# Conformer and short-convolution decoder layer in float32: three gate units placed behind the convolutions, swish as one activation, LayerNorm over eleven units

## What is computed

```
z = rmsnorm(h, norm_g); proj = z @ w_in            # 9 blocks of 1024 columns
a_val, a_glu, a_gate, b_h, b_c, b_b, b_gate, m_a, m_b = split(proj)
u_a = a_val * sigmoid(a_glu)
c_a = layernorm(causal_dwconv31(u_a) + conv_a_b, ln_a_g, ln_a_b)
y_a = silu(c_a) * silu(a_gate)
y_b = b_b * causal_dwconv3(b_c * b_h) * silu(b_gate)
merged = sigmoid(m_a) * (y_a @ w_pa) + sigmoid(m_b) * (y_b @ w_pb)
y = rmsnorm(h + merged @ w_out, final_norm_g)       # and the convolutions' last rows
```

## Time and profile before

| | |
|---|---|
| median of 3 runs | 1204.2 us (1204.0 to 1205.83) |
| the profiled execution | 1199.34 us |
| its span, first to last instruction | 1197.4 us |
| mean granted TensorE clock | 0.951 |
| TensorE matmul busy | 1059.4 us, 88%, 7948 matmuls |
| VectorE busy | 808.6 us, 68% |
| ScalarE busy | 440.1 us, 37% |
| GpSimd busy | 594.5 us, 50% |
| moved by DMA | 212.24 MB, mean 177 GB/s |

### The profile page before, as it was taken

The page is one execution under the profiler, slowest core; times in us unless marked ns, Lnnn a source line. Parts: engine busy times, 40 slices in busy tenths (PEclk is TensorE's granted clock), DMA queues, the critical chain, the costliest instruction groups (busy, mean ns, idle before and its releaser), DMA issues.

```text
span 1197.4 us, 19916 instructions
## 1 busy us (share of the span) xinstructions
PE 1059.4 (88%) x7948; PEld 1026.6 (86%) x7948; DVE 808.6 (68%) x853; ACT 440.1 (37%) x679; POOL 594.5 (50%) x451
## 2 busy tenths in 40 slices
PE   5869999999999999999999899854969694997997
PEld 4869999999999999999999889854969694996885
DVE  6636867968868999898989675671283286445333
ACT  7343333334334333333333445532443152223221
POOL 2166556656566565666666455532555464455000
PEclk8879999999999999999999999987889897998999
DMA  7355576566667566665766988897767968565220
GB/s 254 104 138 134 133 193 167 147 164 171 146 159 175 145 171 161 159 164 135 177 148 149 246 248 244 257 294 252 180 189 222 269 178 251 162 214 176 89 88 38
DMA packets 217151, 212.24 MB, mean 177 GB/s; under 512 B 10751, under 2 KB 170623, under 8 KB 216020
## 3 DMA queue, kind: packets, MB, share of 16 engines
q1 hardware_dynamic: 192292, 165.87, 43.7%
q0 software_dynamic: 24768, 45.10, 21.1%
HBM read 131.83 MB, written 35.00 MB: 139 GB/s over the span
## 4 chain that ended last, share of the span: by engine, by line
PE 38%; DVE 22%; DMA 15%; issue 10%; POOL 4%; ACT 4%; SPq 3%; DVEq 0%; ACTq 0%; POOLq 0%
PE pp L1835 29%; PE pp L1989 8%; POOL wop L824 4%; DVE spare L1453 3%; DVE big L1442 3%; DMA sgb<-m_spill 3%; DMA big<-c_spill 2%; DMA ya_spill<-big 2%; DVE spare L1442 2%; DMA c_spill<-big 2%; DMA m_spill<-big 2%; DMA ga_spill<-big 1%; DVE big L1492 1%; ACT wop L893 1%; DMA big<-ya_spill 1%
## 5 line engine op out<-in xcount | busy, mean ns | idle before, releaser
L1835 PE MATMUL pp<-xop,wop 128*128 128x262 f32 (+1 forms) x7224 | 916.2, 290 | 105.4 <-ACT big L1053 43.1
L1835 PEld LDWEIGHTS pp<-xop,wop 128*128 128x128 f32 x7224 | 907.3, 194 | 112.2 <-issue 106.7
L824 POOL TENSOR_TENSOR wop<-ring,wop 128x512 fp32r<-128x512 f32 (+1 forms) x262 | 446.3, 1712 | 409.4 <-ACT wop L893 405.5
L893 ACT ACTIVATE wop<-ring 128x512 fp32r<-128x512 f32 (+1 forms) x262 | 181.8, 698 | 268.0 <-PE pp L1835 256.2
L1442 DVE SCALAR_TENSOR_TENSOR big<-big,cst 128x513 f32<-128x513 f32 x112 | 106.9, 955 | 0.4
L1989 PE MATMUL pp<-xop,wop 128*128 128x512 f32 x384 | 91.9, 402 | 6.6 <-DVE wop L1785 6.6
L1989 PEld LDWEIGHTS pp<-xop,wop 128*128 128x128 f32 x384 | 73.8, 193 | 24.5 <-issue 6.8
L1522 DVE TENSOR_TENSOR big<-big,pp 128x524 f32<-128x524 f32 (+1 forms) x43 | 29.9, 695 | 91.5 <-PE pp L1835 91.0
L1453 DVE SCALAR_TENSOR_TENSOR spare<-big,tap_sum,spare 128x512 f32<-128x512 f32 x112 | 83.8, 748 | 0.3
L1442 DVE SCALAR_TENSOR_TENSOR spare<-big,cst,spare 128x512 f32<-128x512 f32 x112 | 83.6, 747 | 0.0
L1349 DVE TENSOR_TENSOR xop<-big,xop 128x2064 fp32r<-128x2064 f32 (+1 forms) x21 | 55.3, 2639 | 24.7 <-ACT xop L919 24.6
(11 more groups left out here) (126 smaller groups left out, 700.1 us busy)
## 6 DMA issues: line engine op xcount, KB each, us to landing
ring<-in_w_in_dram SPq DMA_DIRECT2D x249, 256.0 KB, 3.4
ring<-ring POOLq DMA_DIRECT2D x172, 256.0 KB, 4.6
big<-c_spill SPq DMA_DIRECT2D x16, 516.0 KB, 5.2
ring<-in_w_pb_dram SPq DMA_DIRECT2D x28, 256.0 KB, 3.9
ring<-in_w_pa_dram SPq DMA_DIRECT2D x28, 256.0 KB, 3.9
big<-yb_spill SPq DMA_DIRECT2D x5, 1032.0 KB, 7.4
big<-ya_spill SPq DMA_DIRECT2D x5, 1032.0 KB, 12.7
yb_spill<-big SPq DMA_DIRECT2D x8, 516.0 KB, 5.4
```

The source lines that it names most:

```text
L824: G.tensor_tensor(wop[:, s0:s1, 1, :], raw, f(wop[:, s0:s1, 0, :]), ALU.subtract).then_inc(wlo, 1)
L893: A.activation(wop[:, s0:s1, 0, :], raw, ACT.Copy).then_inc(whi, 1)
L1835: last = T.matmul(out, wop[:, s, wp, P * k:P * (k + 1)], xop[s][:, xp, k, n * ch:n * (ch + 1)], start=(s in FRESH and k == 0 and m == 0), ...
```

## The change

- `agate` 1 to 3 leave their places behind `gate` 0, 1 and 2 and stand between `mix` 3 and `mix` 4. Units 1 to 24 are now the 24 units of the convolution blocks and 25 to 35 are eleven "late" units, n = 0 to 10: `mix` 0 to 3, `agate` 1 to 3, `mix` 4 to 7. All blocks use the former `TIGHT` table.
- Every swish is one ScalarE instruction with the function Silu; the VectorE multiplications by the sigmoid go.
- LayerNorm steps are placed by n from 0 to 8, with four `nrm` buffers for three and finer steps; the quarter loads of phase 1 stand at n = 9, in the order 2, 3, 0, 1. Operand steps of the `pb` and `pa` phases move earlier by one or two places, and in the first `pa` unit the merge stands behind `c12`.

```diff
     for j in range(K):
         UNITS += [("glu", j), ("short", j), ("gate", j)]
-        if j < 3:
-            UNITS += [("agate", j + 1)]
-    UNITS += [("mix", q) for q in range(K)]
+    LATE0 = len(UNITS)
+    UNITS += [("mix", q) for q in range(4)] + [("agate", m) for m in range(1, 4)] + [("mix", q) for q in range(4, 8)]
...
-        nrm = [cut(TOK * (2 + i), TOK) for i in range(3)]
+        nrm = [cut(TOK * i, TOK) for i in (2, 3, 4, 7)]
...
-        SPREAD = {"short": (2, 9, 11, 13), "gate": (13, 20, 22, 23), "agate": (25, 33, 35, 36), "end": (38, 44, 46, 48)}
-        TIGHT = {"short": (3, 13, 15, 17), "gate": (17, 25, 27, 29), "end": (31, 42, 44, 48)}
+        SPREAD = {"short": (3, 13, 15, 17), "gate": (17, 25, 27, 29), "end": (31, 42, 44, 48)}
...
-                if u == M + 6:
-                    spill_ya(7)
-                    for q in range(4):
-                        load_quad(1, q)
+                if n == 9:
+                    for q in (2, 3, 0, 1):
+                        load_quad(1, q)
+                if u == NZ + 1:
+                    for q in (2, 3, 0, 1):
+                        load_quad(2, q)
...
                 elif kind == "gate":
-                    act.wait_ge(ub_ready, 2 * i + 1)
-                    A.activation(half(g2, u, 0), src, ACT.Sigmoid).then_inc(bsig_ready, 1)
+                    A.activation(src, src, ACT.Silu).then_inc(bswish_ready, 1)
...
             def norm_swish(j):
-                row = nrm[(8 + j) % 3]
                 act.wait_ge(ys_step, 2 * j + 2)
-                wait(act, ya_step, 2 * j - 1)
-                A.activation(nsig, row, ACT.Sigmoid, scale=const(j, C_LNG), bias=const(j, C_LNB))
-                A.activation(row, row, ACT.Identity, scale=const(j, C_LNG), bias=const(j, C_LNB)).then_inc(nsig_ready, 1)
+                A.activation(nrm[j % 4], nrm[j % 4], ACT.Silu, scale=const(j, C_LNG), bias=const(j, C_LNB)).then_inc(nswish, 1)
...
-                if kind == "gate":
-                    dve.wait_ge(bsig_ready, 2 * i + 1)
-                    V.tensor_tensor(half(g2, u, 0), half(g2, u, 0), half(g1, u, 0), ALU.mult).then_inc(yb_step, 1)
...
-                if u == NZ:
-                    x_sum(1, 2)
-                    x_low(1, 2)
-                    x_low(1, 3)
+                if u == NZ:
+                    x_low(1, 4)
...
+                    if n == 4 and s == 3:
                         pe.wait_ge(mean_ready, 3)
                         pe.wait_ge(sqacc, K)
                         column_mean(rstd, 0, None, var_t)
                         column_mean(rstd, 1, None, var_t)
-                    if u == M + 3 and s == 0:
+                    if n == 4 and s == 4:
                         column_mean(rstd, 2, std_ready, var_t)
```

More of the change, by code:

```diff
@@ L74, in decoder_step, with late @@
     NZ, NPB, NU = 36, 40, 44
-    MIX0, LAST = NZ - K, NU - 1
-    assert len(UNITS) == NU and UNITS[MIX0] == ("mix", 0) and UNITS[NZ] == ("pb", 0)
+    LATES, LAST = NZ - LATE0, NU - 1
+    assert len(UNITS) == NU and UNITS[NZ] == ("pb", 0)
+    def late(u):
+        return u - LATE0 if LATE0 <= u < NZ else -1
     AT = {unit: u for u, unit in enumerate(UNITS)}
@@ L307, in p_buf @@
         def p_buf(u):
-            return {"glu": g1, "short": g2, "gate": g1}.get(UNITS[u][0], g3)
+            return {"glu": g1, "short": g2, "gate": g2}.get(UNITS[u][0], g3)
         def q_buf(u):
@@ L642, in _ @@
                 ahead = u + 2 < NU
+                n, last_n = late(u), late(u - 1)
                 if ahead:
@@ L651, in _ @@
                     load_states(i)
-                if last_kind == "mix":
-                    spill_mix2(last_i)
-                if u == M + 1:
+                if last_n >= 0:
+                    spill_p2(last_n)
+                if n == 3:
+                    load_c(7)
+                if n == 6:
+                    spill_ya(1)
+                    load_ga(3)
+                if n == 7:
+                    spill_ya(3)
+                    load_ga(5)
+                if n == 8:
+                    spill_ya(5)
+                    load_ga(7)
+                if n == 9:
[4 more added lines that the diff above has]
+                        load_quad(2, q)
+                if u and u + 1 < NU:
+                    load_u4(u + 1)
+                if last_n >= 0:
+                    spill_q(last_n)
+                if last_kind == "glu" and last_i > 0:
+                    spill_c(last_i - 1)
+                if n == 1:
                     spill_c(K - 1)
@@ L991, in first_product @@
                 kind, i = UNITS[u]
+                n = late(u)
                 if u == 1:
@@ L1580, in after_c21 @@
                 kind, i = UNITS[u]
-                if kind in ("short", "gate", "agate", "pb", "pa"):
+                if kind in ("short", "pb", "pa"):
                     dve.wait_ge(prod, prod_at(u, 6))
```

615 lines of the change are left out of this document (290 added, 325 removed).

## The result

The changed kernel takes 1175.33 us (median of 4 runs, 1172.79 to 1175.67), the kernel before 1204.1 us beside it: a ratio of 0.9755, 95% interval 0.9737 to 0.9772. It is 29 us faster where 76 were forecast, and lies 1.3 us above the range. The profiled execution took 1175.6 us with a span of 1173.8.

The account below looks back on a forecast made before the run. TensorE's idle gaps and slower clock behind them were the loss, with transfers bounding the late units. Start 118.5, convolution 454.1, late 260, `pb`/`pa` 178, tail 110.9, plus 1.9: 1123.4; plus 4.9 is 1128.3 us, range 1096 to 1174.

Parts of the forecast that it names:

- I take 118.5 as it is: Start, units 0 to 2: about 1.4 us saved by removed multiplications against a 1.28 us table load, so 118.5 us stays.
- Convolution units, 454.1: Units 3 to 24: TensorE's 0.73 us wait for `c22` goes, 61.9 us a block, 22 x 20.64 = 454.1 us.
- 2.1 us of cover remain: `gate` units: despite the table load, ScalarE's copy of slot 3 ends 2.1 us before TensorE needs it; loads cost nothing.
- Table-load rival: ScalarE's copies are as tight everywhere as in unit 1: 22 x 1.28 = 28 us more, 1156 us; chance 0.12.
- each unit to run as unit 30 did: Late units 25 to 35: transfers bound, ten units at unit 30's 23.6 us plus 20.5 is 256.5; sum taken 260 us.
- at the average: `mix` 6's unit, heavier than 6.1 MB with quarter loads ahead of Q's store, and lighter `mix` 7: pair left at average.
- transfer rival: Late units: DMA engines stay over 0.9 busy and ten units take 28.6 us each, 1178 us in all; chance 0.16.
- `pb` and `pa`, 178: Units 36 to 43: gaps removed, times 1.3 for the slower clock, save 40 us of 218.4, leaving 178 us.
- The 6.85 us goes: `pb` and `pa`: three operand steps of slots 2 to 4 move from unit 36 to unit 35, removing a 6.85 us gap.
- the 13.38 goes: Unit 40: merge stands behind `c12` and the last operand ahead of `c22`, removing a 13.38 us gap.
- the 7.31 only halves: Unit 37: phase 2's quarter loads still stand ahead of a needed store and load, so the 7.31 us gap halves.
- Half of the other 14.2: `pb` and `pa`: half of the remaining 14.2 us of gaps, 7.1 us, goes, as several follow an operand step.

Follow-up runs that it names:

- dup_no_table: dup_mult with Sigmoid in place of Silu, so no table load stands between two activations of a gate unit, the extra VectorE operation kept: 1181.8 us.
- dup_mult: The changed kernel with one VectorE operation of the removed multiplication's size and place put back in each of the eight gate units: 1216.1 us.
- no_table: The changed kernel with Sigmoid for every Silu (factor x left out), so 23 of the 28 table loads go: 1173.4 us.
- q_earliest: The changed kernel with Q made before P's second half and stored in its own unit, ahead of the load L427: 1154.1 us.
- thin_reads: The changed kernel without seven eighths of LayerNorm's reads (c and gate rows), same queue order and count of transfers: 1156.7 us.

## Why the prediction was wrong

- **Start, "I take 118.5 as it is": wrong by 3.9.** The table load is where the forecast put it, and costs its 1.28 us. ScalarE in unit 1, to be read against the earlier trace rows:

```profile
86.95 0.63 ACT L906 ACTIVATE wop<-ring 128x512 fp32r<-128x512 f32 x1 [4.33 <-DMA ring<-ring]
87.60 1.28 ACT L1077 ACT_TABLE_LOAD   x1
88.90 0.64 ACT L1077 ACTIVATE big<-big 128x524 f32<-128x524 f32 x1
89.44 1.93 ACT L932 ACTIVATE xop<-big 128x2096 fp32r<-128x2096 f32 x1
```

  The 1.4 us set against it bought nothing: the weight copy at 86.95 (85.66 before) waits for a weight sum, which landed 1.3 us later than before although all up to it ran 1.4 us earlier. Why it landed later stays open. The forecast also left out the slower clock: the 96 matmuls behind the wait took 14.62 us, at a granted clock of 0.79, where the earlier trace rows has 11.97 at 1.00. Other kernels with the same start reached `c12` of unit 2 at 119.5 to 121.9 us, so the true miss may be as small as 1.
- **Convolution units, 454.1: right**, by its mechanism: no `c22` wait in any `gate` unit, 62.1 us a block. dup_no_table puts the removed multiplication at 0.72 us of TensorE's wait a block (0.73 taken). "2.1 us of cover remain" was right for ScalarE's copy. The forecast did not see that VectorE would have had no cover at all, had its multiplication stayed (dup_mult).
- **Table-load rival (28 us): wrong**; no_table gives 2.
- **Late units, "each unit to run as unit 30 did", 23.6 us: the step that failed first.** The forecast read share 0.91 and 259 GB/s in unit 30 as a bound by bytes. It was not: q_earliest's unit 31 moves 6.6 MB in 20.5 us, more than the 6.1 of unit 30, and TensorE does not stand. The 2.8 us in which TensorE stood in unit 30 were two waits for ScalarE's copies (L1053 and L1060), each behind a squaring of LayerNorm (L1146) that waited for VectorE. ScalarE and TensorE in unit 30 of the kernel before:

```profile
708.97 1.07 ACT L1146 ACTIVATE big<-big 128x1032 f32<-128x1032 f32 x1 [2.89 <-DVE big L1624]
710.07 0.61 ACT L1053 ACTIVATE big<-pp 128x524 f32<-128x524 f32 x1
...
713.70 1.06 ACT L1146 ACTIVATE big<-big 128x1032 f32<-128x1032 f32 x1 [1.97 <-DVE big L1624]
```

```profile
710.82 3.16 PE L1835 MATMUL pp<-xop,wop 128*128 128x262 f32 x24 [1.34 <-ACT big L1053]
...
715.40 3.16 PE L1835 MATMUL pp<-xop,wop 128*128 128x262 f32 x24 [1.42 <-ACT big L1060]
```

  The changed kernel waits for something else, the store of Q, with more transfers ahead of it: it was issued 2.3 us after Q was made in unit 30 before, and 5.0 us after in unit 31 now. The bytes themselves were summed rightly (65.6 MB; 278.0 us at 235 GB/s are 65.3). Units 26 to 35 took 25.7 us on average in the changed kernel and 22.5 to 23.3 in the best ones. Of the 18 us, 13 stand in unit 34, which the text knew to be heavy and left "at the average"; the four quarter loads ahead of the store had cost 16.30 us in the earlier trace rows and cost 13.24 again. The other five are the small waits for the same store. The 3 us for the variance were right (3.09).
- **The transfer rival (1178)** came within 3 us of the time, but by luck: it puts 50 us more into the late units, where 18 stood, and had nothing for the last phases. By thin_reads bytes do have a part in it, but it named only the rate and not the place in the queue.
- **`pb` and `pa`, 178: the largest miss, 32.5.** "The 6.85 us goes", "the 13.38 goes" and "the 7.31 only halves" each took away what a wait of before was for, and did not ask what now stands ahead in the same list. In their places stand 10.30 and 9.81 us (the operand of slot 6 ahead of the copy of slot 2), 10.56 (the store behind the quarter loads) and 5.66 (`c22` of unit 39). VectorE's half of that operand was visible in the order of instructions ahead of the prediction: it stands ahead of `c22` and waits for ScalarE's copy (`xhi`). "Half of the other 14.2" had no row behind it. The lower bound of 168 was not there either: with all of these orders mended the phases take 193 to 207 us, and 183 with most of GpSimd's subtractions left out. The forecast has no term for GpSimd beside VectorE; the runs do not price it exactly.
- **The 4.9 us from the profiled execution to the median: wrong.** The changed kernel's profiled execution lies at its median. That term was one execution's luck and should have been in the range alone.
- **Tail: right** (110.0 for 110.9).

## What to carry to other kernels

An idle engine is not cover for an instruction that waits: price a move by what will stand behind the moved instruction on each in-order list, ScalarE's, VectorE's and the DMA queue's, while it waits for its slowest input. A high DMA share shows that bytes are in flight, not that they bound: at a share of 1.02 TensorE did not stand in unit 31 of q_earliest, and at 0.99 it stood 3.75 us in unit 31 of the changed kernel. Look at when a store is issued against when its data was ready, and at what ended each wait in the unit that serves as the model. And when two parts of a change touch the same step, cost each with and without the other: here one costs 5 to 8 us, one 2, and both over 40.
